# 512-column records for the u tiles that run beside the selection tables

## The reference

```python
gates = sigmoid(g + b_gate)                     # three branches of 1024 columns each
merged = gates[0]*ya + gates[1]*yb + gates[2]*yc
...
v1, i1 = top_k(s1, 16); v2, i2 = top_k(s2, 16)  # per token and head, over 128 + 128 keys
top, ci = top_k(v1[:, None] + v2[None, :], 16)
idx = i1[ci // 16] * 128 + i2[ci % 16]
gate = softmax(top)
act = gelu(einsum('td,tkd->tk', xb, expert_u[idx]))
out = einsum('tk,tkd->td', gate * act, expert_v[idx])
```

## Time and profile before

| | us |
|---|---|
| median of three runs | 2027.26 |
| the profiled execution, its own time | 2030.79 |
| its span | 2028.9 |
| TensorE matmul busy | 2003.4 (99%) |
| VectorE busy | 1534.6 (76%) |
| ScalarE busy | 1054.6 (52%) |
| GpSimd busy | 1030.9 (51%) |

### The profile page before, as it was taken

One profiled execution on the slowest core, in us unless ns is written; L12 is line 12 of the kernel. 1 busy time (PEld: TensorE's weight loads), 2 busy tenths in 40 slices (PEclk: granted clock), 3 DMA queues, 4 the chain that ended last, 5 costly groups with the idle time before them and its releaser, 6 DMA issues.

```text
span 2028.9 us, 39016 instructions
## 1 busy us (share of the span) xinstructions
PE 2003.4 (99%) x12276; PEld 1793.8 (88%) x12276; DVE 1534.6 (76%) x3160; ACT 1054.6 (52%) x1730; POOL 1030.9 (51%) x425
## 2 busy tenths in 40 slices
PE   9999999999999999999999999999999999999998
PEld 7998788899999888888889988888999998888887
DVE  1866369988887888888638653799888878888886
ACT  5644455567776333333466444555677753333333
POOL 6799779787775000000268898797777740000001
PEclk9999999999999999999999999999999999999999
DMA  8455557676665777777774555576656668777875
GB/s 247 134 195 186 177 185 234 211 229 197 196 196 194 245 241 241 241 240 241 238 218 136 187 182 198 196 236 211 217 197 198 195 206 244 242 240 242 241 243 174
DMA packets 172124, 429.56 MB, mean 212 GB/s; under 512 B 19156, under 2 KB 83957, under 8 KB 171510
## 3 DMA queue, kind: packets, MB, share of 16 engines
q1 hardware_dynamic: 171588, 425.56, 66.1%
q10 hardware_dynamic: 434, 2.63, 0.3%
HBM read 392.79 MB, written 35.32 MB: 211 GB/s over the span
## 4 chain that ended last, share of the span: by engine, by line
PE 76%; POOL 10%; issue 8%; DVE 3%; ACT 1%; DMA 1%; POOLq 0%; DVEq 0%; ACTq 0%; SPq 0%
PE bank L1599 33%; PE bank L1321 20%; POOL halves L547 10%; PE bank L1585 9%; PE bank L1587 5%; PE bank L1650 3%; PE bank L1343 3%; PE bank L1345 1%; DMA ring<-in_stream 1%; PE bank L1565 1%; DVE area L1176 0%; DVE area L1180 0%; DVE area L1183 0%; DVE area L933 0%; ACT halves L628 0%
## 5 line engine op out<-in xcount | busy, mean ns | idle before, releaser
L547 POOL TENSOR_TENSOR halves<-ring,halves 128x1024 fp32r<-128x1024 f32 x412 | 1025.3, 2502 | 976.6 <-DVE coef L1264 682.9
L628 ACT ACTIVATE halves<-ring 128x1024 fp32r<-128x1024 f32 x668 | 704.9, 1056 | 707.0 <-PE bank L1599 412.4
L1599 PE MATMUL bank<-halves,coef 128*128 128x512 f32 x3000 | 681.4, 389 | 0.0
L1599 PEld LDWEIGHTS bank<-halves,coef 128*128 128x128 f32 x3000 | 562.6, 188 | 117.5 <-issue 0.5
L1321 PE MATMUL bank<-hT,halves 128*128 128x256 f32 x4512 | 565.7, 283 | 0.2
L1321 PEld LDWEIGHTS bank<-hT,halves 128*128 128x128 f32 x4512 | 552.2, 192 | 2.2 <-issue 0.7
L1244 DVE TENSOR_TENSOR halves<-ring,halves 128x1024 fp32r<-128x1024 f32 x256 | 315.6, 1233 | 10.2 <-ACT halves L628 10.2
L1585 PE MATMUL bank<-hT,halves 128*128 128x512 f32 x896 | 311.4, 393 | 3.1 <-POOL halves L547 3.1
L1587 PE MATMUL bank<-hT,halves 128*128 128x256 f32 x896 | 249.5, 279 | 0.0
L1585 PEld LDWEIGHTS bank<-hT,halves 128*128 128x128 f32 x896 | 167.8, 187 | 41.3 <-issue 3.7
L1343 PE MATMUL bank<-hT,halves 128*128 128x512 f32 x512 | 181.3, 399 | 1.7 <-DVE hT L922 1.7
(11 more groups left out here) (174 smaller groups left out, 1704.7 us busy)
## 6 DMA issues: line engine op xcount, KB each, us to landing
ring<-in_stream SPq DMA_DIRECT2D x668, 512.0 KB, 3.9
held_blocks<-act SPq DMA_DIRECT2D x244, 128.0 KB, 1.8
act<-held_blocks SPq DMA_DIRECT2D x244, 128.0 KB, 3.0
area<-rel_scratch SPq DMA_DIRECT2D x16, 128.0 KB, 6.3
area<-in_gains SPq DMA_DIRECT2D x4, 512.0 KB, 4.8
x_home<-x ACTq DMA_DIRECT2D x2, 1024.0 KB, 3.9
x<-x_home SPq DMA_DIRECT2D x2, 1024.0 KB, 8.1
area<-in_params SPq DMA_DIRECT2D x2, 640.0 KB, 7.7
```

The costliest lines, as they stand in the source:

```text
L547: pool.tensor_tensor(halves[:, s, 1, :], ring[:, s, :], halves[:, s, 0, :].bitcast(F32), ALU.subtract)\
L628: a.activation(halves[:, s, 0, :], ring[:, s, :], ACT.Copy).then_inc(hi_done, 1)
L1599: i = pe.matmul(acc[2 * t + hf][:, :], coef[:, k, a, t * P:(t + 1) * P], halves[:, s, e, hf * HALF_N:(hf + 1) * HALF_N], start=opens and n ...
```

## The change

Three things change. The 68 u tiles beside and behind the tables use `sided` into one of two banks: ScalarE copies one half of the bank into the block's buffer (`half`), VectorE adds the other half (`add_halves`), and ScalarE applies the gelu in place (`finish`). ScalarE now scales three of the four one-hot rows of a set, and VectorE one. Gate group 5 of the mixer goes back to 24 matmuls of 256 columns, and its sums on VectorE go away. Around this some steps move: the exponentials of the softmax stand behind the high part of a tile, not ahead of it; VectorE adds one more parked tile inside the search; and the first set of one-hot rows is built before the last parked tile is added.

```diff
-PLAIN = 2
+SUMMED = (2, 3, 4)
+PLAIN = (0, 1, 5)
...
-                a.wait_ge(shifted_ready, l + 1)
-                a.activation(sel[:, 2], sel[:, 2], ACT.Exp).then_inc(gexp_ready, 1)
-                a.activation(stat[:, 13:14], one, ACT.Gelu_apprx_tanh)
-                with a.Fori(EXP_AT, PARKED // RING - 1) as r:
+                for r in range(EXP_AT, PARKED // RING - 1):
                     for s in range(RING):
-                        turn(r, s)
+                        if r == EXP_AT and s == 0:
+                            a.wait_ge(tiles_used, l * NT + r * RING + (T_PU + s + 1))
+                            high(r * RING + (T_PU + RING + s), s)
+                            a.wait_ge(shifted_ready, l + 1)
+                            a.activation(sel[:, 2], sel[:, 2], ACT.Exp).then_inc(gexp_ready, 1)
+                            a.activation(stat[:, 13:14], one, ACT.Gelu_apprx_tanh)
+                            park(r, s)
+                        else:
+                            turn(r, s)
...
-                def hold(i):
+                def half(i):
 
                     a.wait_ge(tiles_used, l * NT + (T_HU + i + 1))
+                    a.wait_ge(held_stored[i % 2], l * (8 * (EARLY - 2)) + (8 * PARKED + 16 * (i // 2 + 1)))
+                    a.activation(act[:, i % 2, :], bank_u[i % 2][:, S:], ACT.Copy).then_inc(half_copied, 1)
                     high(T_HU + RING + i, i % RING)
-                    a.wait_ge(held_stored[i % 2], l * (8 * (EARLY - 2)) + (8 * PARKED + 16 * (i // 2 + 1)))
-                    gelu(i % 2)
...
-                    for u in range(2, FOUR):
+                def finish(i):
+
+                    a.wait_ge(halves_added, l * BESIDE + i + 1)
+                    a.activation(act[:, i % 2, :], act[:, i % 2, :], ACT.Gelu_apprx_tanh).then_inc(act_done, 1)
...
-                a.wait_ge(weights_hi, 2 * l + 2)
-                weighted(0)
                 for n in range(SETS):
-                    if n >= 1:
-                        side(2 * n - 2)
-                        side(2 * n - 1)
+                    half(n)
+                    if n == 0:
+                        a.wait_ge(act_done, l * NK + PARKED)
+                    side(2 * n)
+                    side(2 * n + 1)
+                    finish(n)
                     if n + 1 < SETS:
                         weighted(n + 1)
-                    hold(n)
...
                 link(v.tensor_scalar(cb.rearrange("p t h j -> p (t h j)"), ci.rearrange("p t h j -> p (t h j)"), 15, None,
                                      ALU.bitwise_and))
+                fold()
...
                 onehots(0)
+                fold()
                 onehots(1)
-                for n in range(1, SETS):
-                    if n + 1 < SETS:
-                        onehots(n + 1)
-                    add_side(2 * n - 2)
-                    add_side(2 * n - 1)
-                add_side(NQ - 2)
-                add_side(NQ - 1)
+
+                def add_halves(i):
+
+                    v.wait_ge(half_copied, l * BESIDE + i + 1)
+                    v.tensor_tensor(act[:, i % 2, :], act[:, i % 2, :], bank_u[i % 2][:, 0:S], ALU.add).then_inc(halves_added, 1)
+
+                for n in range(SETS):
+                    add_halves(n)
+                    if n + 2 < SETS:
+                        onehots(n + 2)
+                    add_side(2 * n)
+                    add_side(2 * n + 1)
+                for i in range(HELD, BESIDE):
+                    add_halves(i)
...
                     else:
-                        pe.wait_ge(act_done, l * NK + (PARKED + i - 1))
-                    u_product(i % RING, i % 2)
+                        pe.wait_ge(halves_added, l * BESIDE + i - 1)
+                    sided(i % RING, bank_u[i % 2])
```

More of the change, by code:

```diff
@@ L117 @@
     + [("pT0", "A")] * 2 + [("pT1", "A")] * 4 + [("attn", "A")] * 4 + [("gmlp", "V")] * 2 + [("pool", "V")] * 2
-    + [step for kind, n in MIX[1:] for step in ([("branch", "V")] * 2 if kind == "branch" else [("gate", "A")] * 2 if n < PLAIN else [("sum", "V")] * 4)]
+    + [step for kind, n in MIX[1:] for step in ([("branch", "V")] * 2 if kind == "branch" else [("gate", "A")] * 2 if n not in SUMMED else [("sum", "V")] * 4)]
     + [("wo", "V")] * 3 + [("h2T", "V")] * 2 + [("wo", "V")] + [("h2T", "V")] * 2 + [("qq", "V")] * 2 * PH + [("score", "A")] * 8
@@ L202, in program @@
         stat = sb("stat", [P, 20])
-        weight = sb("weight", [P, SETS, 2])
+        weight = sb("weight", [P, SETS, FOUR - 1])
         used = [0]
@@ L371, in program @@
         sides_added = sem("sides_added")
+        half_copied = sem("half_copied")
+        halves_added = sem("halves_added")
         sig_done = sem("sig_done")
@@ L718, in gates @@
                         high_up_to(T_GATE[n] + 2 * k + 1 + 3)
-                        if n < PLAIN:
+                        if n not in SUMMED and n >= 3 and k == 0:
+                            a.wait_ge(taken_v, l * NGV + taken_before(place("branch", 2 * (n - 2) + 1) + 1)[0])
+                        if n not in SUMMED:
                             b = group("gate")
@@ L724, in gates @@
                             into = sig_of(n)[:, 2 * k + c, :]
[L725 to L728, removed]
+                            if n in SUMMED:
+                                a.wait_ge(taken_v, l * NGV + taken_before(place("sum", 4 * (n - SUMMED[0]) + 2 * k + c) + 1)[0])
+                            i = a.activation(into, b[:, c * S:(c + 1) * S] if n not in SUMMED else into, ACT.Sigmoid, bias=par[:, col:col + 1])
+                        i.then_inc(sig_done, 1) if n in SUMMED else i.then_inc(taken_a, 1)
                 gates(0)
@@ L785, in turn, with weighted @@
                     park(r, s)
+                def weighted(n):
+                    a.wait_ge(low_placed, l * SETS + n + 1)
+                    for u in range(1, FOUR):
+                        rows = onehot2[:, n % 2, u, 0, :]
+                        i = a.activation(rows, rows.bitcast(F32), ACT.Copy, scale=weight[:, n, u - 1:u])
+                    i.then_inc(onehots_ready, 1)
                 with a.Fori(0, EXP_AT) as r:
@@ L827, in side @@
                         .then_inc(side_copied, 1)
-                a.wait_ge(weights_hi, 2 * l + 2)
-                weighted(0)
                 for n in range(SETS):
-                    if n >= 1:
-                        side(2 * n - 2)
-                        side(2 * n - 1)
+                    half(n)
[4 more added lines that the diff above has]
+                    finish(n)
                     if n + 1 < SETS:
                         weighted(n + 1)
-                    hold(n)
[L838 to L841, removed]
+                for i in range(HELD, BESIDE):
+                    half(i)
+                    finish(i)
                 with a.Fori(0, EARLY // RING) as r:
@@ L1643, in _ @@
                     pe.wait_ge(onehots_ready, l * SETS + n + 1)
+                    if n == 0:
+                        pe.wait_ge(sides_added, (l + 1) * PARKED)
                     for q in (2 * n, 2 * n + 1):
```

31 lines of the change are left out of this document (14 added, 17 removed).

## The result

The changed kernel takes 2049.76 us (median of three executions; the kernel before beside it 2026.53, median of four). The ratio of the two kernels is 1.0104, with a 95% interval from 1.009 to 1.0118. Run once more on another chip it took 2047.75 us beside 2029.48, 1.0092 times (1.0076 to 1.0109). So it is slower by about 1%, 18 to 23 us, where the forecast was 4.6 us slower and its range ended at 2038. One more execution (3375.81 us, its clock at 0.60) was disturbed and is left out.

What follows compares the result with a forecast made beforehand. TensorE, busy 99% of the span, was taken as the bound, with ScalarE's chain limiting the table stretch. Layer terms (-2.2 - 0.65 + 2.97 + 0.38) gave +1.0 us for two layers, clock +3.6: +4.6, about 2032 us, range 2021 to 2038.

Steps and rivals of the forecast that it cites:

- Gate group 5: Mixer: four tiles go from 2.83 to 2.92 us, +0.38 us a layer; VectorE's four lost sums count nothing.
- The loop: Table stretch, 63 periods a layer: each falls from 3.36 to 3.325 us, every other set waiting about 0.15 us.
- the chain: ScalarE's ordered work in a table-stretch set, from copying half to the next set's scalings: 3.05 us.
- The tile: A u tile in 512-column records takes 2.77 us on TensorE, as in the parked stretch, instead of 2.88.
- the tile is longer: Table-stretch rival: chain 0.1 us longer or tile 2.83 us, either +4 to +6 us, 2037 in all; chance 0.13.
- the gain of 2.2 us a layer: Table stretch: 63 periods, each shorter by 0.035 us, save 2.2 us a layer.
- The forecast's own sum: Table stretch, two sets: TensorE period 3.25, then 0.16 + 0.04 + 3.05 + 0.15, together 6.65 us.
- my bound of 3.25: Table stretch: the period is never under TensorE's own 3.25 us a set, a gain of 6.9 us a layer.
- The end of the stretch: Last u tiles to first v matmul: TensorE waits for VectorE's addition and low part, +2.97 us a layer.
- The start: Selection to first one-hots: rows come in time but VectorE's extra addition delays the transposes, net -0.65 us a layer.
- The clock: Half-clock falls behind TensorE's new pauses: 2 to 3 falls in 4 pauses, +3.6 us in all, bounds 0 and 6.8.
- the 4 pauses of the forecast: TensorE waits in each of two layers: 2.8 us ahead of the selection, 3.3 us ahead of the v stage.

Runs made afterwards that it cites:

- the three experiments on it: Changed kernel with gate group 5 in 512-column records: 1.0046; kernel before with only gate group 5 plain: 1.0046; changed kernel with bank rotation moved by two: 1.0051.
- the weighting moved: Changed kernel with ScalarE's scaling of the next set's one-hot rows put right behind the high part, ahead of side copies and gelu: 1.0052.
- the kernel with the reduction: Changed kernel with the high part of the merged rows written by a VectorE reduction over a one-element axis instead of a copy: 1.0084.

## Why the prediction was wrong

- **Gate group 5: the step that failed.** "VectorE loses four sums that nobody waits for: nothing", and 0.38 us a layer in all. The price of the four tiles themselves was near (11.31 to 11.52 us, +0.2 where I had 0.38). But the edit takes two groups out of a rotation that every later group shares, and TensorE waits at w_out for a bank, which it had not done: 3.2 us of idleness a layer, and the clock at half behind it. By the three experiments on it, it costs 8 to 12 us. It was to be read before the run: PLAN loses two groups, the function that gives the bank counts them, and VectorE's product in the row at 192.67 above ends 5.5 us after TensorE has begun w_out. I counted what the edit issues and not what it renumbers.
- **The loop.** The mechanism was right, the chain too (3.05 forecast, 3.07 measured). The tile was mis-sized: 2.83 us, not 2.77. The parked stretch has tiles of 2.77, the loop doesn't. That is the rival "the tile is longer", and the gain of 2.2 us a layer was none. The forecast's own sum with this tile, 3.31 + 0.16 + 0.04 + 3.07 + 0.15 = 6.73 us for two sets, is what was measured. With the weighting moved, 2.83 + 0.48 = 3.31 is what TensorE takes, so my bound of 3.25 is not reached in any run.
- **The end of the stretch.** +2.97 forecast, +2.98 and +3.18 measured: right.
- **The start.** -0.65 forecast. The wait ahead of the selection is 2.1 and 2.9 us (2.8 forecast), that for GpSimd is gone, and layer 1 gives -0.73 from the parked tiles to the first one-hots. In layer 0 the parked tiles took 2.83 us each instead of 2.77, and the parked stretch 155.0 us where layer 1 took 152.9, +2.1 us. Windows of 120 us of the changed kernel, layer 0 and layer 1 (length, busy (x matmuls), clock, DMA share, GB/s):

```profile
280.00:400.00 120.00, 120.00 (x681) 1.00 0.70 229
1290.00:1410.00 120.00, 120.00 (x695) 1.00 0.68 224
```

- **The clock.** 2 to 3 falls in the 4 pauses of the forecast at about 1.45 us; 2 came in each of the two profiles. Over all kernels with these pauses the clock fell behind 10 of 20 at the selection (2.1 to 2.9 us) and behind 10 of 16 at the v stage (3.3 us), which is 2.2 of 4. The size was near, too (1.6 us): the v stage takes 345.8 us without a fall and 347.4 with one of 3.4 us. What was missing is the third pause, at w_out, behind which it fell every time.

Summed: forecast +4.6; add 9 for w_out, 4.7 for the loop that gained nothing, and 2 for the slow parked tiles of one layer, and it is about 20, within the 18 to 23 measured. The last term is chance: it is in the profiled execution, and most layers of the other kernels don't have it.

## What to carry to other kernels

An edit that changes how many groups, tiles or buffers are taken from a rotation shifts everything behind it. So before pricing the instructions, list for each later user who had its buffer last, before and after, and when that reader is done. A pause of TensorE should be priced with the clock behind it, which cost nearly as much here as the pause; it is cheapest to order the other engines' last steps so that no pause arises, and where one stays, spare matmuls in it hold the clock. And a chain on an engine that is idle for a quarter of the time can still close the ring: look whether what the bottleneck waits for stands last in that engine's order.

## What the runs showed of the hardware

- A VectorE copy or an operation with two operands in SBUF, 128x512, ended 0.3 or 0.55 us behind the end of the GpSimd instruction that ran when it started, and so took 1.0 to 2.8 us. The reduction (0.69, beside GpSimd in the kernel with the reduction) and the product with an operand in PSUM (0.68, at 192.67 in the kernel before) did not stop.
- The clock fell behind 14 of 14 pauses of 2.7 to 3.4 us at w_out, and behind 20 of 36 of 2.1 to 3.3 us elsewhere. In layer 1 of the changed kernel it held behind 2.9 us and in layer 0 behind 3.3. Such a fall lasted 3.4 or 6.8 us, and the stage was 1.5 to 1.7 or 2.6 to 2.9 us longer. Three more falls stand at the start of the query stage, one of them in the kernel before, behind several waits of 0.8 to 1.3 us close together.
- The same u tile took 2.77 or 2.83 us in the parked stretch, one or the other for a whole layer (2.83 in four of the 28 layers profiled), at full clock and with no wait. In the loop it was always 2.83. The query stage in the same way took 51.5 or 52.4 us at full clock. What sets either stays open; the first is worth 2 us a layer.
